# A fused two-block transformer kernel on one core: a shorter last normalisation, the first two query tiles interleaved by pieces, the choice's scores moved behind one tile

## The reference

```
def rms_norm(x, g):
    y = x * lax.rsqrt(jnp.mean(x * x, axis=-1, keepdims=True) + EPS)
    return y * g

def peer_ffn_2(h, w_pq, peer_keys, peer_u, peer_v):
    q = (ht @ w_pq).reshape(T, 8, 2, 128)                 # queries, 2048 columns
    sub = jnp.einsum('thpc,hpnc->thpn', q, peer_keys)     # scores against 128 keys, 16 times
    ...                                                   # top 16 of each half, top 16 of their sums, softmax
    act = gelu(einsum('cd,ckd->ck', xc, u))               # kernel: dense, all 16384 experts
    return einsum('ck,ckd->cd', gate * act, vv)

x = x + gt2[:, None, :] * peer_ffn_2(h2, ...)
return rms_norm(x, g_final)                               # the last step of the kernel
```

## Time and profile before

| | |
|---|---|
| median of 3 runs | 2192.66 us (2191.41 to 2193.33) |
| the profiled execution's own time | 2192.78 us |
| its span | 2190.9 us |
| PE busy | 2143.4 us (98%) |
| DVE busy | 1572.7 us (72%) |
| ACT busy | 1268.0 us (58%) |
| mean granted clock of PE | 0.991 |

### The profile page before, as it was taken

How to read it: one execution, slowest core, us unless ns; L and a number is a source line. 1 busy time by engine, 2 the same in 40 slices (tenths; PEclk the granted TensorE clock), 3 DMA queues, 4 the chain that set the end, 5 groups by cost and what they waited for, 6 DMA issues and landing times.

```text
span 2190.9 us, 37734 instructions
## 1 busy us (share of the span) xinstructions
PE 2143.4 (98%) x14372; PEld 1941.7 (89%) x14372; DVE 1572.7 (72%) x3423; ACT 1268.0 (58%) x2364; POOL 103.9 (5%) x136
## 2 busy tenths in 40 slices
PE   7999999999999999999999998999999999999998
PEld 5988899898999988888889998999999998888886
DVE  3455658888888867888866655688888887555556
ACT  3355545546999754445545544454579996545554
POOL 0000000404000000000000000004040000000000
PEclk9999999999999999999989999999999999999999
DMA  8665556656443467778744634566554445555664
GB/s 335 204 205 184 176 188 182 191 184 187 127 132 126 156 201 281 283 275 291 255 145 135 204 95 135 184 185 192 183 174 133 127 126 173 182 193 193 193 193 133
DMA packets 110498, 407.49 MB, mean 186 GB/s; under 512 B 11504, under 2 KB 11888, under 8 KB 110064
## 3 DMA queue, kind: packets, MB, share of 16 engines
q1 hardware_dynamic: 98880, 361.81, 51.2%
q10 hardware_dynamic: 11440, 43.28, 5.2%
HBM read 403.99 MB, written 1.05 MB: 185 GB/s over the span
## 4 chain that ended last, share of the span: by engine, by line
PE 91%; DVE 3%; ACT 2%; POOL 2%; issue 1%; DMA 1%; ACTq 0%; DVEq 0%
PE PB L464 24%; PE PB L466 23%; PE PB L465 23%; PE PB L830 6%; PE PB L860 5%; PE PB L858 3%; POOL AR L2303 2%; PE PB L531 1%; PE PB L857 1%; PE PB L802 1%; PE PB L545 1%; PE PB L510 1%; ACT WH L1153 0%; DMA X<-in_x 0%; DVE WL L1604 0%
## 5 line engine op out<-in xcount | busy, mean ns | idle before, releaser
L1604 DVE TENSOR_TENSOR WL<-RING,WH 128x1024 fp32r<-128x1024 f32 x651 | 803.0, 1234 | 477.3 <-ACT WH L1153 475.5
L1153 ACT ACTIVATE WH<-RING 128x1024 fp32r<-128x1024 f32 x651 | 686.6, 1055 | 457.2 <-PE PB L466 454.8
L464 PE MATMUL PB<-HX,WH 128*128 128x256 f32 x2112 | 615.0, 291 | 6.8 <-DVE HX L1659 6.0
L466 PE MATMUL PB<-HX,WL 128*128 128x256 f32 x2112 | 599.5, 284 | 0.0
L465 PE MATMUL PB<-HX,WH 128*128 128x256 f32 x2112 | 599.2, 284 | 0.0
L464 PE MATMUL PB<-WH,HX 128*128 128x512 f32 (+2 forms) x1344 | 494.3, 368 | 7.2 <-DVE HX L1659 3.2
L466 PE MATMUL PB<-WH,HX 128*128 128x512 f32 (+2 forms) x1344 | 490.6, 365 | 0.0
L465 PE MATMUL PB<-WL,HX 128*128 128x512 f32 (+2 forms) x1344 | 490.2, 365 | 0.0
L464 PEld LDWEIGHTS PB<-HX,WH 128*128 128x128 f32 x2112 | 407.0, 193 | 13.1 <-issue 10.1
L465 PEld LDWEIGHTS PB<-HX,WH 128*128 128x128 f32 x2112 | 406.7, 193 | 0.4
L466 PEld LDWEIGHTS PB<-HX,WL 128*128 128x128 f32 x2112 | 405.9, 192 | 0.0
(11 more groups left out here) (233 smaller groups left out, 1849.4 us busy)
## 6 DMA issues: line engine op xcount, KB each, us to landing
RING<-in_u SPq DMA_DIRECT2D x256, 512.0 KB, 3.5
RING<-in_v SPq DMA_DIRECT2D x256, 512.0 KB, 4.2
RING<-in_win SPq DMA_DIRECT2D x90, 512.0 KB, 3.6
AR<-in_wm ACTq DMA_DIRECT2D x40, 1024.0 KB, 6.6
RING<-in_wq SPq DMA_DIRECT2D x32, 512.0 KB, 3.5
AR<-in_wm SPq DMA_DIRECT2D x8, 1024.0 KB, 16.1
RING<-in_wout SPq DMA_DIRECT2D x16, 512.0 KB, 3.5
RING<-in_sk SPq DMA_DIRECT2D x8, 512.0 KB, 3.9
```

Of the source, the lines that this page charges most:

```text
L464: e.matmul(o, ah, bh, start=start, stop=False)
L466: return e.matmul(o, al, bh, start=False, stop=stop)
L1153: e.activation(hi(t), raw(("w", t), words(t)), ACT.Copy).then_inc(s_hi, 1)
L1604: e.tensor_tensor(lo(t), raw(("w", t), words(t)), hi(t).bitcast(F32), ALU.subtract).then_inc(s_lo, 1)
```

## The change

There are four edits. In the tail of block 1, DVE no longer makes XG. Its functions `last_sums` and `last_rows` make the sums and the reciprocal as before, and then one operation per 512 columns multiplies X by the reciprocal and by the weight. The first row half's sums stand between the third and the fourth bank, and ACT's root for it stands behind ACT's third square. The output leaves in four transfers of 256 KB. In both blocks, the first two query tiles are computed together: for each of the four pieces, PE runs two k steps of the first tile and two of the second, and s_used rises by two at the end. `scores(0)` stands at j = 1, behind the first u tile, with its waits for s_qv and s_qa. The ring entries of `scores(1)` stand one tile earlier in PLAN.

```diff
@@ fetch_plan
-            if j == 39:
+            if j == 38:
                 plan.extend([("s", 4 * blk + 2), ("s", 4 * blk + 3)])
@@ sync_program
-            for a in range(2):
-                e.wait_ge(s_fin, a + 1)
-                e.dma_start(out.rearrange("(a p) d -> a p d", p=128)[a], OUT[:, a, :]).then_inc(s_out, 16)
-            e.wait_ge(s_out, 32)
+            for i in range(4):
+                a, cs = i // 2, slice(512 * (i % 2), 512 * (i % 2) + 512)
+                e.wait_ge(s_fin, i + 1)
+                e.dma_start(out[128 * a:128 * a + 128, cs], OUT[:, a, cs]).then_inc(s_out, 16)
+            e.wait_ge(s_out, 64)
@@ tensor_program
+            def first_pair(b, n, h0):
+                ws = [[t.rearrange("p (k n) -> p k n", k=KT) for t in (hi(n + j), lo(n + j))] for j in range(2)]
+                tile_ready(e, n + 1)
+                for kp in range(4):
+                    e.wait_ge(s_hl, h0 + kp + 1)
+                    for j in range(2):
+                        wh, wl = ws[j]
+                        for k in (2 * kp, 2 * kp + 1):
+                            r = three(PB[b][:, 256 * j:256 * j + 256], wh[:, k, :], wl[:, k, :], HH[:, k, :], HL[:, k, :],
+                                      (j, k) == (0, 0), (j, k) == (1, KT - 1))
+                r.then_inc(s_used, 2)
...
-                    half(1 + c % 3, 0, n_q + 2 * c, h0 if c == 0 else None)
+                    if c == 0:
+                        first_pair(1, n_q, h0)
+                        continue
+                    half(1 + c % 3, 0, n_q + 2 * c)
                     half(1 + c % 3, 1, n_q + 2 * c + 1)
-                e.wait_ge(s_qv, 4 * blk + 4)
-                e.wait_ge(s_qa, 4 * blk + 4)
-                scores(0)
...
+                    if j == 1:
+                        e.wait_ge(s_qv, 4 * blk + 4)
+                        e.wait_ge(s_qa, 4 * blk + 4)
+                        scores(0)
                     if j == 39:
                         scores(1)
@@ scalar_program
                         square(X[:, a, cs], a, h, 512).then_inc(s_sq, 1)
+                        if i == 6:
+                            root(5, 0, 1)
...
-            for a in range(2):
-                root(5 + a, a, a + 1)
+            root(6, 1, 2)
@@ vector_program
                         e.tensor_tensor(X[:, a, cs], X[:, a, cs], UW[:, i, :], ALU.add).then_inc(s_tx, 1)
-                        e.wait_ge(s_tx, 4 * blk + i + 1)
-                        e.tensor_tensor(XG[:, a, cs], X[:, a, cs], FG[:, cs], ALU.mult).then_inc(s_tg, 1)
+                        if blk == 0:
+                            e.wait_ge(s_tx, i + 1)
+                            e.tensor_tensor(XG[:, a, cs], X[:, a, cs], FG[:, cs], ALU.mult).then_inc(s_tg, 1)
+                        elif i == 2:
+                            last_sums(0)
+                        elif i == 3:
+                            last_rows(0)
+                            last_sums(1)
+                            last_rows(1)
+
+            def last_sums(a):
+                e.wait_ge(s_sq, 27 + 2 * a)
+                own.done(own.mark(e.tensor_reduce(ST[:, 24 + a:25 + a], ST[:, 8 + 4 * a:10 + 4 * a], AX, ALU.add)))
+                e.tensor_scalar(ST[:, 26 + a:27 + a], ST[:, 24 + a:25 + a], 1.0 / D, EPS, ALU.mult, ALU.add).then_inc(s_ms, 1)
+
+            def last_rows(a):
+                e.wait_ge(s_rt, 6 + a)
+                own.done(own.mark(e.reciprocal(ST[:, 30 + a:31 + a], ST[:, 28 + a:29 + a])))
+                e.wait_ge(s_tx, 6 + 2 * a)
+                for h in range(2):
+                    cs = slice(512 * h, 512 * h + 512)
+                    e.scalar_tensor_tensor(out=OUT[:, a, cs], in0=X[:, a, cs], scalar=ST[:, 30 + a:31 + a], in1=FG[:, cs],
+                                           op0=ALU.mult, op1=ALU.mult).then_inc(s_fin, 1)
...
-            for a in range(2):
-                mean_squares(5 + a, 27 + 2 * a, 2, a, a + 1)
-                e.wait_ge(s_tg, 6 + 2 * a)
-                scaled(OUT, XG, a, 30 + a).then_inc(s_fin, 1)
```

## The result

| | before | after |
|---|---|---|
| median of nine runs each, us | 2191.35 (2190.72 to 2193.33) | 2184.76 (2184.09 to 2188.18) |
| ratio, 95% interval | | 0.9970 (0.9962 to 0.9978) |
| profiled execution, us | 2192.78 | 2186.88 |
| its span, us | 2190.9 | 2185.0 |
| mean granted TensorE clock in it | 0.991 | 0.991 |

The change makes the kernel 0.3% faster, 6.6 us by the medians and 5.9 us by the two traces. The forecast was 2187.1 with a range of 2185.0 to 2190.0; the measured 2184.76 lies 0.24 us under its low end. The forecast was wrong in size and right in direction.

What follows compares the result with a forecast made beforehand. PE was taken as the bound, busy 98% of the span, with DVE and the transfer setting the end. Gains of 2.01 + 0.71 + 0.25 + 1.78 + 0.81 = 5.56 us turned 2192.78 into 2187.22, median 2187.1, range 2185.0 to 2190.0.

Steps and rivals of the forecast that it cites:

- the base: Whole kernel: the starting time is the profiled execution, 2192.78 us, with the median of the runs 0.12 below.
- tail, DVE: End of block 1: DVE's last operation ends at 2186.51 against 2187.87, 1.36 us gained (0.6 to 1.6).
- tail, landing: Output store: the last transfer is half as large, so 0.65 us of its 2.6 us landing goes.
- pair, block 0: First query pair of block 0: no hole is left between PE's 48 matmuls, 0.71 us gained.
- pair, block 1: First query pair of block 1: hole and its slower first matmul go, 0.25 us at equal clock (0.12 to 0.4).
- scores(0), two blocks: Ahead of scores(0): PE's 0.89 us idle for ACT's copy goes in each block, 1.78 us together.
- keys: Ahead of scores(1): keys come 2.88 us sooner, so lateness of 0.34 and 0.47 goes, 0.81 us (0.49 to 0.9).
- (a): Output tail: last transfer isn't shorter and the new operation takes its upper end, about 2187.9 us; chance 0.12.
- (c): Behind scores(0): PE waits at the second or third u or fourth query tile, about 2189.2 us; chance 0.10.
- (d): Both blocks: the choice runs a tile late throughout, late low parts stop PE, 2198.6 us; chance 0.03.
- (b): Ahead of a block's first pair: one more low-clock stretch, costing 1.7 us, 2188.8 (or 2185.4 if it goes); chance 0.13.

Runs made afterwards that it cites:

- b2x: Kernel before, unchanged, run again for a third trace; 2191.14 us, ratio 0.9995 (0.9985 to 1.0005).
- x1_two: Changed kernel with its output in two transfers of 512 KB instead of four; 2185.74 us, ratio to before 0.9972 (0.9960 to 0.9984).
- k1_keys: Kernel before with only the ring entries of scores(1) one tile earlier; 2189.66 us, ratio 0.9991 (0.9982 to 1.0000).
- d4x: Kernel before with 4 throwaway matmuls (0.88 us) among block 0's v tiles; 2192.35 us, ratio 1.0002 (0.9993 to 1.0011).
- w2b: Kernel before with 13, 9 and 4 throwaway matmuls where PE idles around block 1's norms and first pair; 2189.66 us, ratio 0.9994 (0.9985 to 1.0003).
- w2a: Changed kernel with 13, 9 and 4 throwaway matmuls where PE idles around block 1's norms and first pair; 2181.83 us, ratio to before 0.9956 (0.9942 to 0.9969).
- a1_again: Changed kernel, unchanged, run again; 2184.53 us (2184.24 to 2185.04), ratio to before 0.9966 (0.9952 to 0.9979).
- p3x: Kernel before with only the first pair by pieces, plus 3 throwaway matmuls (0.66 us) among block 0's v tiles; 2192.61 us, ratio 0.9999 (0.9990 to 1.0008).
- p1_pair: Kernel before with only the first query pair by pieces, in both blocks; 2191.47 us, ratio 1.0000 (0.9991 to 1.0009).

## Why the prediction missed

**The step that failed is the base.** "The median of the runs stands 0.12 below it" took the profiled execution, 2192.78, for a typical one, on three runs that were 1.9 us apart. With nine runs before's median is 2191.35, 1.43 below the profiled execution. That is 1.3 of the 2.34 us by which the forecast is too high, and the range had nothing for it: 2191.35 - 5.56 is 2185.8, inside the range. The other 1.0 is the sum of the change, below. The traces show where an execution can be late: the one of `b2x` took 2190.47, and all of the 2.3 us between the two lie ahead of the first pair, a stretch that no term of the forecast looked at. After's profiled execution lies 2.12 above its median.

**The sum of the change, point by point** (us, from the traces; 6.35 against 5.56, and 0.44 given back):

| term | forecast | measured | |
|---|---|---|---|
| tail, DVE | 1.36 | 1.48 | new operation 0.75 as taken, sums covered |
| tail, landing | 0.65 | 0.62 | `x1_two`: 0.6 |
| pair, block 0 | 0.71 | 0.73 | |
| pair, block 1 | 0.25 | 0.51 | bounds were 0.12 to 0.4; not all the edit's, see below |
| scores(0), two blocks | 1.78 | 1.94 | the 0.89 twice, and the scores 0.08 quicker each |
| keys | 0.81 | 1.07 | above its bound of 0.9 |
| start, block 0's end, norm of block 1 | 0 | -0.44 | clock, and one wait for WL of 0.65 |

The mechanisms all held: no hole in the pair, no idle ahead of the scores, the sums behind PE's last nine matmuls, no new wait behind scores(0). Two sizes were off. The keys' wait depends on the execution (0.3 to 1.1 us in total in all eleven traces with the old order of the keys, before three times and eight kernels built on it), and one trace cannot bound it; `k1_keys` gave 1.7 in the median. The pair of block 1 was valued "at equal clock", while half of it ran at 0.52. Its measured 0.51 is in part the clock's: in before two low stretches of 3.4 us lie in the norm and in the pair, in after there is one of 10.2 that ends in the pair. `k1_keys` and `d4x` have the old pair and that one long stretch; from the norm's transposes to scores(0), less the tile that now stands ahead of the scores, they are only 0.06 and 0.2 us longer than after. So at the low clock the edit is worth 0.1 to 0.2 us there, about the low end of the forecast, and with the clock held up 0.74 (`w2b` to `w2a`), more than its bounds. The scores gave 0.16 more than forecast.

**The rivals.** (a) fell: landing 2.0. (c) and (d) did not occur: there is no wait behind scores(0), and scores(1) to the 48 matmuls is no longer than before. (b) was the right kind of rival, but named one place of two. Around block 1's norm and pair the low clock rose from 6.8 us to 10.2, and at block 0's end it fell from 13.7 to 10.2. What counted was which matmuls it met: at block 0's end its place alone made 0 to 1.47 us between the kernels. The price of (b), 1.7 us for 3.40 us of low clock, is also a little high: by the earlier trace rows 16 matmuls ran in that time, which take 1.92 at 0.12 each, so 1.5 were lost. The new wait for WL at 1121.55 comes with the clock too: it is in every trace in which at most 3.4 us are low behind the start of those tiles, and in none with 5.1 or more.

**What stays open.** The medians differ by 6.6 us and the traces from the first pair on by 6.0; the ratio's interval goes from 4.8 to 8.3 us in these terms, so the last 0.6 cannot be told from nothing, although `a1_again` at an equal mean clock is again 6.7 under before. Part of it may be how often each kernel has the late start of 13.7 us of low clock, but this was not counted over runs. Why `p3x` does not follow its trace is not settled.

## What to carry to other kernels

Before a forecast of a few tenths of a per cent, put the base on more runs than the profiled one, which here stood 1.4 us above the median, a quarter of the forecast effect. Value each removed wait by its rows, then ask which matmuls lie in the next low stretch of the clock: an edit that gains nothing alone (the pair, the scores) may have only moved that stretch, and can be worth keeping in company. Split the last store, whose landing nothing covers, and fill PE's idle time ahead of a low stretch with a number of matmuls whose time is measured, not reckoned. Here that gave 3.0 us at block 1's norm and nothing at block 0's end, where DVE was late.

## What the runs showed of the hardware

- Counted from the 48 one-column matmuls, the granted clock falls at nearly the same place in every trace of one program (4.1 to 4.7 us in three of before, 3.5 us in two of after), and under 1 us of other work moves it to 2.4 us (`p1_pair`) or back to 4.7 (`p3x`). Ahead of the first pair the low time differs between traces of one program (13.7 and 10.2 us). The one-column matmuls keep PE busy for 5.94 of 6.47 us in before, and the clock falls within them all the same.
- The mean granted clock of a run goes with its time. In the 111 runs of before that stood beside the experiments: 2191.24 on the mean at 0.992 (81 runs), 2192.72 at 0.991 (17), 2194.44 at 0.990 (5), 2195.58 at 0.989 (8). Seven of after's nine runs and all five of `a1_again` were at 0.992 or 0.993.
- A filling matmul (`ones` by `ident`, 128 x 128 by 128 columns) showed as two records and took 0.22 us at the full clock, while those of line 465, with 256 columns, start 0.12 apart.
- A multiplication of 128 x 512 f32 by a scalar per row and by a second input took 0.750 us, against 0.69 for the plain product. The Trainium skill, "VectorE: DVE Perf Modes", section "The perf-mode tier table (the rule you actually need)", holds tensor_tensor on f32 at the single rate and tensor_scalar at twice that; it has no row for this form. The trace puts it with tensor_tensor: the old one-input form covered twice the elements in the same 0.75.
